# A layer kernel on one core: its first stage rebuilt on a transposed input from the host

## The reference, cut to what matters

```python
def rms_norm(x, g):
    y = xf * lax.rsqrt(jnp.mean(xf * xf, axis=-1, keepdims=True) + EPS)
    return (y * g.astype(jnp.float32)).astype(x.dtype)
...
    proj = xn @ w_in
    lx, lg, q, k, v, rg, ga, gb = jnp.split(proj, split_idx, axis=-1)
    xp = jnp.concatenate([conv_state.astype(lx.dtype), lx], axis=1)
    xc = conv_b + sum(xp[:, j:j + L] * conv_w[j] for j in range(CONV_WIDTH))
...
    log_a = -LRU_C * r * jax.nn.softplus(-lru_lambda.astype(f32))
```

## Time and profile before

| | us |
|---|---|
| median of 3 runs | 1895.08 (1893.64 to 1899.26) |
| the profiled execution, its own time | 1896.27 |
| its span in the trace | 1894.3 |
| slot 1's first matmul (start of the second block on PE) | 49.41 |
| slot 0's second product begins | 62.51 |
| PE busy over the span | 1776.6 (94%) |

### The profile page before, as it was taken

One profiled execution on the slowest core, in us unless ns is written; L12 is line 12 of the kernel. 1 busy time (PEld: TensorE's weight loads), 2 busy tenths in 40 slices (PEclk: granted clock), 3 DMA queues, 4 the chain that ended last, 5 costly groups with the idle time before them and its releaser, 6 DMA issues. The chain is left out here.

```text
span 1894.3 us, 25704 instructions
## 1 busy us (share of the span) xinstructions
PE 1776.6 (94%) x10104; PEld 1549.2 (82%) x10104; DVE 1049.5 (55%) x1225; ACT 781.4 (41%) x943; POOL 493.4 (26%) x286
## 2 busy tenths in 40 slices
PE   5999999999999999999999979959999999999992
PEld 4999989999899999999899968847777766666661
DVE  6555680001455445554611142458888888898884
ACT  5455460000122111221300022237788777777774
POOL 1323232322322222222223210012334322232210
PEclk8999999999999999999999989979999999999996
DMA  4211111223111111111122446438999999999995
GB/s 132 62 51 44 33 55 61 68 69 123 40 45 33 36 36 47 36 33 36 51 88 91 168 160 251 177 103 323 368 375 377 369 368 363 364 363 374 371 334 200
DMA packets 146085, 316.17 MB, mean 167 GB/s; under 512 B 10652, under 2 KB 106092, under 8 KB 121292
## 3 DMA queue, kind: packets, MB, share of 16 engines
q1 hardware_dynamic: 136140, 288.27, 42.2%
q0 software_dynamic: 9856, 26.66, 5.2%
HBM read 287.46 MB, written 35.29 MB: 170 GB/s over the span
## 5 line engine op out<-in xcount | busy, mean ns | idle before, releaser
L220 PE MATMUL job_ps<-xn_hi,w_hi 128*128 128x352 f32 x1536 | 511.7, 333 | 3.2 <-PEq L287 2.5
L222 PE MATMUL job_ps<-xn_hi,w_lo 128*128 128x352 f32 x1536 | 495.0, 322 | 0.0
L221 PE MATMUL job_ps<-xn_lo,w_hi 128*128 128x352 f32 x1536 | 494.6, 322 | 0.0
L220 PEld LDWEIGHTS job_ps<-xn_hi,w_hi 128*128 128x128 f32 x1536 | 290.0, 189 | 6.9 <-issue 2.9
L204 POOL CAST w_hi<-w_raw 128x1024 fp32r<-128x1024 f32 x80 | 88.8, 1110 | 782.7 <-issue 468.5
L221 PEld LDWEIGHTS job_ps<-xn_lo,w_hi 128*128 128x128 f32 x1536 | 290.6, 189 | 2.3
L222 PEld LDWEIGHTS job_ps<-xn_hi,w_lo 128*128 128x128 f32 x1536 | 290.1, 189 | 0.0
L2127 DVE TENSOR_TENSOR ex_w_lo<-u,ex_w_hi 128x2048 fp32r<-128x2048 f32 x96 | 218.0, 2287 | 26.2 <-ACT ex_w_hi L2037 26.1
L2127 DVE TENSOR_TENSOR ex_w_lo<-h_raw_more,ex_w_hi 128x2048 fp32r<-128x2048 f32 x96 | 217.7, 2285 | 21.1 <-ACT ex_w_hi L2037 21.0
L2037 ACT ACTIVATE ex_w_hi<-u 128x2048 fp32r<-128x2048 f32 x96 | 183.8, 1917 | 70.2 <-DMA u<-in_w_chunks 32.6
L2037 ACT ACTIVATE ex_w_hi<-h_raw_more 128x2048 fp32r<-128x2048 f32 x96 | 184.5, 1923 | 68.4 <-DMA h_raw_more<-in_w_chunks 36.6
(11 more groups left out here) (286 smaller groups left out, 3056.7 us busy)
## 6 DMA issues: line engine op xcount, KB each, us to landing
u<-in_w_chunks SPq DMA_DIRECT2D x96, 1024.0 KB, 18.1
h_raw_more<-in_w_chunks SPq DMA_DIRECT2D x96, 1024.0 KB, 18.4
w_raw<-in_w_in SPq DMA_DIRECT2D x64, 512.0 KB, 4.2
merged_lru<-gate SPq DMA_DIRECT2D x8, 528.0 KB, 5.2
spare<-merged_lru SPq DMA_DIRECT2D x8, 528.0 KB, 5.8
merged<-gate SPq DMA_DIRECT2D x8, 528.0 KB, 5.2
x_tile<-in_x_prompt SPq DMA_DIRECT2D x8, 512.0 KB, 5.1
w_raw<-in_w_lru_o SPq DMA_DIRECT2D x8, 512.0 KB, 4.4
```

The source lines that it names most:

```text
L220: pe.matmul(out, M.w_hi[s][:, k, :], x_hi[:, k, cols], start=(k == 0), stop=False)
L221: pe.matmul(out, M.w_hi[s][:, k, :], x_lo[:, k, cols], start=False, stop=False)
L222: mm = pe.matmul(out, M.w_lo[s][:, k, :], x_hi[:, k, cols], start=False, stop=(k == KD - 1))
```

## The change

The host also lays out two more inputs: `x_columns` [3, 128, 8, 352], which is the input already turned (feature in block on the partition, per column), and `par_columns` [128, 120], all the parameter vectors with features on partitions, now with `norm_mix_g`. The norm then needs no transposes. It works in place in `R.u`, column by column:

- SP loads the parameters, column 0 of x in two halves of 704 KB (`k` 0 to 3, `k` 4 to 7), the two first weight blocks, columns 1 and 2, and the constants.
- ACT squares a half (L325 of the new kernel). PE multiplies the squares with a matrix of ones in fp32, eight matmuls of 352 tokens (L300), so that every partition of `nm_total` holds the sum over features. ACT takes the root (L331, 352 wide); DVE inverts it (L391, 352 wide) and scales the eight `k` blocks (L393). ACT makes `xn_hi`, DVE `xn_lo`, both in halves of four `k`.
- The first weights are split by ACT (`w_hi`) and DVE (`w_lo`), no longer by POOL.
- DVE's parameter chain runs at the start, while x is on its way; two dummy activations on ACT load tables early, and three matmuls on ones run on PE before the first squares.
- The first products of both slots are made column by column in the order (slot 0, c), (slot 1, c); the sums of column 2 stand behind both products of column 0.
- `normalise` no longer has a block: it returns streams as the other stages do, and is the first of them. `lru` leaves out its `product(1, 0)`. Its `w_gates` buffer lies at another place.

```diff
-        self.psum = [self.bank_set(ctx, 0)]
+        self.psum = [self.bank_set(ctx, s) for s in range(2)]
...
+    def sync(sp):
+        def load(c):
+            for m, ks in enumerate(HALVES):
+                sp.dma_start(x[:, c, ks, :], A["x_columns"][c][:, ks, :]).then_inc(x_in[c][m], 16)
+
+        sp.dma_start(R.par[:], A["par_columns"]).then_inc(par_in, 16)
+        load(0)
+        for s in range(2):
+            J.load(sp, s, 0, following[s])
+        load(1)
+        load(2)
+        sp.dma_start(R.const[:], A["const_small"]).then_inc(const_in, 16)
...
+        pe.wait_ge(set_done, 1)
+        for _ in range(3):
+            pe.matmul(total[1][:], ones[:, 0:P], ones[:], start=True, stop=True)
+        sums(0)
+        sums(1)
+        for c in range(CT):
+            for s in range(2):
+                column(s, c)
+            if c == 0:
+                sums(2)
+        pe.wait_ge(const_in, 16)
...
+        square(0)
+        act.activation(warm[:, 1:2], R.eps[:], ACT.Sqrt)
+        for s in range(2):
+            act.wait_ge(M.raw_in[s], 16)
+            act.activation(M.w_hi[s][:], M.w_raw[s][:], ACT.Copy).then_inc(M.hi_done[s], 1)
+        root(0)
+        square(1)
+        hi(0)
+        root(1)
+        square(2)
+        hi(1)
+        root(2)
+        hi(2)
...
+        for s in range(2):
+            dve.wait_ge(M.hi_done[s], 1)
+            dve.tensor_tensor(M.w_lo[s][:], M.w_raw[s][:], M.w_hi[s][:].bitcast(F32),
+                              ALU.subtract).then_inc(M.split_done[s], 1)
+        for c in range(CT):
+            r = rms[c % 2]
+            dve.wait_ge(rms_done, c + 1)
+            st.link(dve.reciprocal(r[:], r[:]))
+            for k in range(KD):
+                ins = dve.scalar_tensor_tensor(out=x[:, c, k, :], in0=x[:, c, k, :],
+                                               scalar=R.par[:, PR_GMIX + k:PR_GMIX + k + 1], in1=r[:],
+                                               op0=ALU.mult, op1=ALU.mult)
+                if k % 4 == 3:
+                    ins.then_inc(xn_done, 1)
+            for m, ks in enumerate(HALVES):
+                dve.wait_ge(hi_done, 2 * c + m + 1)
+                dve.tensor_tensor(M.xn_lo[:, ks, cols(c)], x[:, c, ks, :], M.xn_hi[:, ks, cols(c)].bitcast(F32),
+                                  ALU.subtract).then_inc(lo_done, 1)
...
         for n in range(KD):
-            J.product(pe, 1, n, M.xn_hi, M.xn_lo)
+            if n:
+                J.product(pe, 1, n, M.xn_hi, M.xn_lo)
...
-            normalise(nc, A, R, Jobs(M, 0), (block("w_in", 0), block("w_in", 1)))
-            M.psum.append(M.bank_set(mixer, 1))
+            nm = normalise(nc, mixer, A, R, Jobs(M, 0), (block("w_in", 0), block("w_in", 1)))
...
-            stages = (ru, ml, rt, mr)
+            stages = (nm, ru, ml, rt, mr)
```

More of the change, by code:

```diff
@@ new lines, in normalise @@
+        total = [ctx.enter_context(nc.psum_tensor(f"nm_total{b}", [P, 512], F32)) for b in range(2)]
+        par_in, const_in = sem("par_in"), sem("const_in")
+        x_in = [[sem(f"x_in{c}{m}") for m in range(2)] for c in range(CT)]
+        set_done = sem("set_done")
+        sq_done, summed = sem("sq_done"), sem("summed")
+        rms_done, xn_done = sem("rms_done"), sem("xn_done")
+        hi_done, lo_done = sem("hi_done"), sem("lo_done")
+        abs_done, exp_done = sem("abs_done"), sem("exp_done")
@@ new lines, in gpsimd, with tensor, sums, column @@
+    def gpsimd(pool):
+        pass
+    def tensor(pe):
+        def sums(c):
+            if c == 2:
+                pe.wait_ge(rms_done, 1)
+            for k in range(KD):
+                if k % 4 == 0:
+                    pe.wait_ge(sq_done, 2 * c + k // 4 + 1)
+                mm = pe.matmul(total[c % 2][:, 0:CW], ones[:, 0:P], sq[c % 2][:, k, :], start=(k == 0), stop=(k == KD - 1))
+            mm.then_inc(summed, 1)
+        def column(s, c):
+            J.column(pe, s, 0, c, M.xn_hi, M.xn_lo,
+                     before_k=lambda k: pe.wait_ge(lo_done, 2 * c + k // 4 + 1) if k % 4 == 0 else None)
+        pe.wait_ge(set_done, 1)
[9 more added lines that the diff above has]
+        pe.wait_ge(const_in, 16)
@@ new lines, in scalar, with square, root, hi @@
+    def scalar(act):
+        def square(c):
+            if c == 2:
+                act.wait_ge(summed, 1)
+            for m, ks in enumerate(HALVES):
+                act.wait_ge(x_in[c][m], 16)
+                act.activation(sq[c % 2][:, ks, :], x[:, c, ks, :], ACT.Square).then_inc(sq_done, 1)
+        def root(c):
+            act.wait_ge(summed, c + 1)
+            if c == 2:
+                act.wait_ge(xn_done, 2)
+            act.activation(rms[c % 2][:], total[c % 2][:, 0:CW], ACT.Sqrt, bias=R.eps[:], scale=1.0 / D).then_inc(rms_done, 1)
+        def hi(c):
+            for m, ks in enumerate(HALVES):
+                act.wait_ge(xn_done, 2 * c + m + 1)
+                act.activation(M.xn_hi[:, ks, cols(c)], x[:, c, ks, :], ACT.Copy).then_inc(hi_done, 1)
+        act.wait_ge(set_done, 2)
+        act.activation(warm[:, 0:1], R.eps[:], ACT.Exp)
+        act.wait_ge(abs_done, 1)
+        act.activation(sp_e[:], sp_a[:], ACT.Exp, scale=-1.0).then_inc(exp_done, 1)
+        square(0)
[11 more added lines that the diff above has]
+        hi(2)
+        act.wait_ge(par_in, 16)
+        act.wait_ge(lam_done, 2)
```

203 lines of the change are left out of this document (49 added, 154 removed).

## The result

The changed kernel takes 1886.95 us (median of 10 runs, 1879.06 to 1889.65) against 1896.11 (10 runs of before, 1892.93 to 1899.26). The ratio on record is 0.9944 with a 95% interval of 0.9933 to 0.9955, 0.56% faster; the two medians alone give 0.9952, a gain of 9.2 us. The forecast was 1884.4 in a range of 1879.5 to 1889.5, a gain of 10.7. Its point is 2.6 us low: the gain is real, of the size of case (a), and the bet on the sign was right. The profiled execution took 1888.79 us, 1.8 above its median, with a span of 1886.1.

A forecast was written before the change was run, and what follows sets the result against it. The prediction took the start to be bound by a chain through DVE and ACT. Bringing slot 0's second product from 62.5 to 51.8 us saves 10.7, so 1896.27 becomes 1885.6 profiled, 1884.4 median; range 1879.5 to 1889.5.

The forecast's parts named there:

- case (a): Forecast case: the mark comes 8 to 13 us earlier, total 1882 to 1887.5 us; chance 0.72.
- The bound and the yardstick: Start is a chain through DVE and ACT; a gain there is worth what it brings forward the mark.
- the mark: PE's first matmul of slot 0's second product, at 62.51 us before, forecast at 51.8.
- The prices: Operation times set from old trace rows, such as 2.5 us for the 352-wide reciprocal and 4.7 for a column's sums.
- The timetable to the first product: Landings, squares, root, reciprocal, scaling and splits at the start; slot 0's column 0 product begins at 21.5 us.
- The 1.65 us for half clock: Added once before the mark, for PE's first products running at half clock after a rest.
- Column 2: Third column's norm chain before the mark: 8.2 us from the end of the sums, with 0.6 us of PE wait.
- the convolution "still hides": DVE's convolution before the gates: 5.5 us, from about 48.7 to 54.2, needed at 55.6, so no wait.
- (b): Reciprocal near 0.45 us or x landing at 370 GB/s: mark at about 47.5, total 1880 us; chance 0.12.
- (c): Start's chain longer (reciprocals, handovers, clock, POOL slowed) or gain eaten later: mark at 57, 1889 to 1892 us; chance 0.10.
- (d): PE at half clock from 21.5 us on: mark at 74, total 1906 us, slower; chance 0.04.
- (e): An engine still waits at the old barrier's place: PE loses 2.5 us, total 1887 us; chance 0.02.

The follow-up runs named there:

- split_late: Changed kernel with POOL beginning slot 1's second weight split only after the first convolution is done; median 1881.42 us, ratio 0.9928 to the kernel before.
- own_block: Changed kernel with the norm put back into a block of its own; median 1892.10 us, ratio 0.9980 to the kernel before.
- slots_in_turn: Changed kernel with all three columns of slot 0's first product ahead of slot 1's; median 1887.32 us, ratio 0.9951 to the kernel before.
- sums2_early: Changed kernel with column 2's sums between slot 0's and slot 1's product of column 0; median 1883.29 us, ratio 0.9929 to the kernel before.
- late_early: Changed kernel with the changes of split_late and sums2_early together, sums in full fp32; median 1880.99 us, ratio 0.9910 to the kernel before.
- no_warm: Changed kernel without PE's three matmuls on ones before the first squares; median 1886.74 us, ratio 0.9939 to the kernel before.
- before_again: The kernel before, unchanged, run again for a second trace; single time 1897.16 us.
- after: The changed kernel itself, against the kernel before; median 1886.95 us, ratio 0.9944.

## Why the prediction was right, step by step

**The bound and the yardstick: right, but for the place of the mark.** The start was a chain through DVE and ACT. Of what the mark gave, 4.4 us were lost right behind it (the step that failed, below); what was left at the second `w_gates` arrived at the end: no trace of a kernel with the new norm ends with less than it had at the second `w_gates`. They end with 2.7 to 9 us more, which the yardstick left out; the shorter rest at retention is part of that, and perhaps the layout.

**The prices: right, nearly all.** The forecast 2.5 us for the 352-wide reciprocal from two short rows measured 2.35. Beyond the 0.157 us of one element that is 6.2 ns for each further one, not 6.6. The estimate from the Trainium skill (VectorE: DVE Perf Modes, "First, the fixed hardware budget"), 2.9 us, is too long by a quarter; the trace decides. Squares 1.37 (1.4), `xn_lo` 1.62 (1.6), fp32 sums 4.89 (4.7), `w_lo` 1.22 (1.2). The scaling was somewhat low: eight take 4.06 us, not 3.6.

**The timetable to the first product: right.** 21.89 against 21.5. The halves of x landed later (5.88 against 5.0, the second at about 7.6 against 7.4), but that didn't move the chain: the two `w_hi`, which waited for no landing, stood ahead of the root and ended at 12.4 as forecast, and the reciprocal began at 13.77 (13.8). The 1.65 us for half clock in the first columns were right in the trace: 9.29 us at 0.82 where two columns and their handovers are 7.6. But it was not a fixed cost: split_late, own_block, slots_in_turn, sums2_early, late_early and no_warm went without, and so did slot 1's product in before_again, the place of the row that the term was read from.

**Column 2: 1 us short.** From the end of the sums' rows (36.07) to its first product (44.83) 8.8 us, not 8.2, most of the excess in the scaling. The sums took 0.2 more than set, the two last columns 8.2 with a short wait instead of 7.9 with handovers. With the 0.4 at the start this puts the mark at 53.06 instead of 51.8, inside case (a).

**The step that failed: the convolution "still hides".** The prediction saw POOL's split fall exactly on the convolution and priced what DVE does to POOL (2.40 to 3.29) but took the convolution at its old 5.5 us. It left out the second split, which POOL makes right behind the first: both weight slots are free within one column now, and in the kernel before the two were 7 us apart (56.61 and 63.95 in the earlier trace rows). The row for the price was there, a scaling of 3.12 us instead of 1.28 beside POOL's `w_lo`; it was used for what the change takes away, not for what it makes. The term should have been 5.5 + about 2 for each `w_lo` in the way = 9.5 us; it measured 9.8 (49.61 to 59.45), the first step too being 0.3 longer (1.10 against 0.83), against an allowance of 7 (from 48.7 to 55.6): a wait of 2.5. Half clock behind it made 1.7 more. Both are shown by split_late.

**The sum.** Forecast 10.7; minus 1.3 (mark), minus 2.5 and 1.7 (convolution) are 5.2, and the trace has 5.0. Plus 3.2 further on makes 8.2, and the medians give 9.2. So the close agreement is in part luck: the forecast missed a cost of 4.2 us at the convolution, which split_late shows, and a gain of 3 to 4 us behind the start, for which no term stood. In the trace of the changed kernel 1.6 of it is a shorter rest at retention, which varies between executions of one kernel, and 2.0 the last quarter, where the layout may be at work. The forecast took the new inputs for free; on the old kernel they were better than that.

**The rivals.** (b) fell with the reciprocal. Of (c), only the collision with POOL came, and it cost time by holding DVE; PE's rest at the mark, where it needs POOL's weights, was 0.27 us. (d), half clock throughout, did not come: half clock showed at two short places, 1.65 and 1.7 us. (e) fell: the streams have no barrier, and own_block shows that a barrier there would cost 5 us, not the 2.5 that (e) gave it. In (d) the break-even is off: at the prediction's own pitches, 0.159 and 0.30, it takes 18 to 20 of the 27.5 us at half clock to be 0.3% slower, not 16.

**Its own signs.** The reciprocal, the pitch of the sums (0.61 us) and column 0's first product came as said. Two did not: PE had two waits over 1 us (1.12 and 2.48), and the later stages were shifted by 5.0 us at the second `w_gates` and 8.2 at the end, not by one amount.

## What to carry to other kernels

Taking away the barrier between two stages is worth more than its own time if the loads and conversions for the second stage can then run under the first; when work is moved across it, ask what covered those before. When two engines' work comes to lie closer together, price the collision in both directions, and count every instruction the neighbour has queued, not only the one that is waited for. And since added inputs and a wider buffer alone were worth 0.2% here, such a share of a gain should be checked on the old kernel with the new layout before it is credited to the idea. A wait of PE of about 2.5 us was followed by up to 1.7 us of half clock in most traces here and by none in some: the cheapest fixes are those that close such rests.

## What the runs showed of the hardware

The 352-wide fp32 reciprocal takes 2.35 us on DVE, against 0.157 us for one element: 6.2 ns for each further one; doubled, it costs 2.4 us each time. A DVE multiply-add with two SBUF inputs that starts inside a POOL subtraction from SBUF waits for its end (3.33 and 3.31 us instead of 1.32). A rest of PE of 2.5 us in the same place was followed by half clock in after (6.73 us for the stretch) and not in sums2_early; with a rest of 1.1 us (column 2 of after) the clock stayed at 1.00. Over all traces of the new norm, the gates' wait of 2.5 us was followed by half clock in five of six; ahead of the first product, rests of 2.7 to 5.1 us were followed by half clock in five of six (late_early, 2.7 us, is the other), and rests of 0.7 to 1.8 us in none of five. Addresses alone moved the whole kernel by 0.23% by the ratio (0.15% by the medians), and the experts' last quarter by 1.7 us in one trace.
